# Four changes of order on VectorE and GpSimd in a two-block transformer kernel

## What is computed

```
# first block
z = n @ w_in[l]                                   # n = rms(h)
...
# second block: the recurrence, per head of 128 keys
fg = lbh + (1.0 - lbh) * jax.nn.sigmoid(heads(f, dk))
logf = jnp.log(fg)
kh = 1.0 - fg
...
b = jnp.cumsum(gc, axis=2)
decay = jnp.where(causal, jnp.exp(jnp.where(causal, diff, 0.0)), 0.0)   # diff = b_t - b_s
a = jnp.einsum('bhtd,bhsd,bhtsd->bhts', qc, kc, decay)
o = o_inter + jnp.einsum('bhts,bhsv->bhtv', a, vc)
...
# cross attention
kv = mem @ wkv                                    # mem is normalised first
```

## Time and profile before

| | |
|---|---|
| median of 3 runs | 1199.69 us (1197.97 to 1202.66) |
| profiled execution | 1202.66 us, span 1200.9 us |
| busy | TensorE 97%, VectorE 58%, ScalarE 48%, GpSimd 48% |
| mean granted TensorE clock | 0.992 |
| DMA | 179.38 MB, mean 149 GB/s |
| forget stage | 553.8 to 590.2 us |
| one pass of the head loop | 65.3 us |

### The profile page before, as it was taken

The page is one execution under the profiler, slowest core; times in us unless marked ns, Lnnn a source line. Parts: engine busy times, 40 slices in busy tenths (PEclk is TensorE's granted clock), DMA queues, the critical chain, the costliest instruction groups (busy, mean ns, idle before and its releaser), DMA issues.

```text
span 1200.9 us, 24182 instructions
## 1 busy us (share of the span) xinstructions
PE 1161.5 (97%) x8692; PEld 1099.9 (92%) x8692; DVE 701.1 (58%) x1326; ACT 573.4 (48%) x1083; POOL 580.1 (48%) x415
## 2 busy tenths in 40 slices
PE   4999999999989999999899999999999989999997
PEld 4999999998879999999899989898889979999996
DVE  4684756685647778427775757666556424444323
ACT  5644444454136665447546454554415344544432
POOL 3666667670035666544563637364105205566541
PEclk9999999999989999999999999999999999999998
DMA  7443344444324455633433433333235415545541
GB/s 288 173 141 141 141 153 154 147 145 148 133 106 141 175 175 175 211 141 108 174 121 116 150 105 122 122 140 140 105 141 210 141 67 200 187 177 186 198 142 35
DMA packets 26061, 179.38 MB, mean 149 GB/s; under 512 B 2832, under 2 KB 3984, under 8 KB 4496
## 3 DMA queue, kind: packets, MB, share of 16 engines
q1 hardware_dynamic: 25712, 177.29, 41.4%
q10 hardware_dynamic: 288, 1.26, 0.3%
HBM read 177.49 MB, written 1.05 MB: 149 GB/s over the span
## 4 chain that ended last, share of the span: by engine, by line
PE 82%; DVE 7%; issue 5%; ACT 2%; POOL 2%; DMA 1%; DVEq 0%; POOLq 0%; SPq 0%; ACTq 0%
PE ps L536 47%; PE ps L478 11%; PE ps L773 10%; PE ps L853 2%; POOL parts L407 1%; PE ps L604 1%; DVE ps L1617 1%; PE ps L503 1%; DVE parts L407 1%; PE ps L576 1%; DVE branch L1816 1%; PE ps L846 1%; PE ps L631 1%; PE ps L649 1%; DVE conv L1850 1%
## 5 line engine op out<-in xcount | busy, mean ns | idle before, releaser
L407 POOL TENSOR_TENSOR parts<-ring,parts 128x1024 fp32r<-128x1024 f32 x184 | 452.1, 2465 | 446.3 <-ACT parts L1031 443.3
L536 PE MATMUL ps<-x_high,parts 128*128 128x256 f32 (+2 forms) x3040 | 411.1, 284 | 3.2 <-DVE parts L407 1.3
L536 PEld LDWEIGHTS ps<-x_high,parts 128*128 128x128 f32 x3040 | 380.8, 188 | 14.5 <-issue 9.8
L1031 ACT ACTIVATE parts<-ring 128x1024 fp32r<-128x1024 f32 x296 | 295.9, 1049 | 118.4 <-PE ps L773 66.9
L407 DVE TENSOR_TENSOR parts<-ring,parts 128x1024 fp32r<-128x1024 f32 x112 | 143.5, 1281 | 131.9 <-ACT parts L1031 131.9
L536 PE MATMUL ps<-x_low,parts 128*128 128x256 f32 (+2 forms) x1520 | 214.5, 284 | 0.0
L536 PEld LDWEIGHTS ps<-x_low,parts 128*128 128x128 f32 x1520 | 196.3, 189 | 0.0
L1617 DVE SCALAR_TENSOR_TENSOR ps<-glu,table_sb,ps 128x256 f32<-128x256 f32 x232 | 93.3, 481 | 0.6 <-DVE ps L1617 0.3
L773 PE MATMUL ps<-act_high,parts 128*128 128x256 f32 x704 | 87.8, 279 | 0.0
L773 PEld LDWEIGHTS ps<-act_high,parts 128*128 128x128 f32 x704 | 85.1, 188 | 0.0
L2127 POOL TENSOR_TENSOR sq<-sq 128x256 f32<-128x256 f32 (+1 forms) x18 | 17.2, 956 | 124.2 <-ACT sq L1007 124.0
(11 more groups left out here) (288 smaller groups left out, 1571.0 us busy)
## 6 DMA issues: line engine op xcount, KB each, us to landing
ring<-weights SPq DMA_DIRECT2D x166, 1024.0 KB, 4.8
table_sb<-table ACTq DMA_DIRECT2D x1, 1102.0 KB, 6.1
res<-h_in SPq DMA_DIRECT2D x4, 272.0 KB, 6.2
act<-mem SPq DMA_DIRECT2D x1, 1024.0 KB, 12.8
out<-xT SPq DMA_DIRECT2D x4, 256.0 KB, 2.4
work<-positions ACTq DMA_DIRECT2D x1, 128.0 KB, 3.3
```

The source lines that it names most:

```text
L407: eng.tensor_tensor(parts[:, LOW - HIGH + p, cols], ring[:, slot, cols], parts[:, p, cols].bitcast(F32), ALU.subtract)\
L536: mm = pe.matmul(out, left(k), right(k), start=step_ == 0 and k == 0, stop=step_ == 2 and k == KB - 1)
L1031: sc.activation(parts[:, p, cols], ring[:, slot, cols], ACT.Copy).then_inc(split_high, 1)
```

## The change

Four places change. None changes what is computed, and no instruction is added or removed.

1. In the first head pass, the eight subtractions of the memory's low parts all stand behind `combine1(0)`; before, four stood ahead of `maxima1(0)`.
2. In the forget stage, the low half of a following chunk is made behind the tensor_scalars of tiles 1, 3 and 5 instead of ahead of them.
3. In the head loop, VectorE makes levels 7 and 8 (the second head's first two) right behind low part 5, then both rope steps, and only then `gather1` and `gather2`. Before: `gather1`, rope, `gather2`, levels 7 and 8.
4. GpSimd clears `kl` behind the low half of the head loop's second chunk instead of ahead of it.

```
-            def x_low_parts(dst, src, high, width, name, tiles=range(KB)):
-                for k in tiles:
+            def x_low_parts(dst, src, high, width, name):
+                for k in range(KB):
...
-                else:
-                    x_low_parts(mem_low, k_mem, mem_high, SEQ, "mem", range(4))
                 maxima1(0)
...
                 combine1(0)
                 if earlier is None:
-                    x_low_parts(mem_low, k_mem, mem_high, SEQ, "mem", range(4, KB))
+                    x_low_parts(mem_low, k_mem, mem_high, SEQ, "mem")
...
             for t in range(KB):
-                if t in (1, 3, 5):
-                    low_v("forget" if t < 4 else "heads2", 0, t // 2 + 2 if t < 4 else t // 2 - 2)
                 b = STREAM.bank("forget", t)
...
                 ve.tensor_scalar(bT[:, t, :], bT[:, t, :], LOG_MIN, None, ALU.max).then_inc(forget_ready, 1)
+                if t in (1, 3, 5):
+                    low_v("forget" if t < 4 else "heads2", 0, t // 2 + 2 if t < 4 else t // 2 - 2)
...
                 low_v("heads2", i, 5)
-                gather1()
+                level(i, 1, 7)
+                level(i, 1, 8)
                 rope_sin(2)
                 rope_cos(k_r)
+                gather1()
                 gather2()
-                level(i, 1, 7)
-                level(i, 1, 8)
                 if scan:
...
-            low_g("heads2", 0, 0)
+            for c in range(2):
+                low_g("heads2", 0, c)
             gp.wait_ge(cum_ready, 2)
             gp.memset(kl, 0.0).then_inc(pool_step, 1)
-            low_g("heads2", 0, 1)
             gp.wait_ge(pool_step, n.next(pool_step))
```

## The result

The changed kernel takes 1214.04 us, the median of four runs (1213.07 to 1215.06), against 1200.33 us for the kernel before, the median of four (1197.97 to 1202.66): 13.7 us more, a ratio on record of 1.0117 with a 95% interval of 1.0105 to 1.013. The profiled spans are 1200.9 and 1212.4 us, 11.5 apart. The four runs of the kernel before scatter by 4.7 us, so the difference is not sharp: 71 further runs of that kernel, made beside the experiments on three chips, have a median of 1202.38, and 29 runs of the changed kernel one of 1214.31, 11.9 more, which fits the profiles better than 13.7 does.

What follows compares the result with a forecast made beforehand. TensorE, busy for the whole 65.3 us of a head-loop pass, was taken to bound the kernel. Terms 2.6 + 0.2 + 0 + 9.6 = 12.4 us on the 1199.69 us median gave 1212.1 us, range 1201.5 to 1220.0.

Steps and rivals of the forecast that it cites:

- the likeliest case: Whole kernel: the forecast itself, 1212.1 us, as a case 1209 to 1215 us, chance 0.45.
- Edit 1, +2.6: First head pass: maxima1(1) starts 5.5 us late, probabilities ready at 59.4 against 56.80, 2.6 us slower; bounds 0 and 3.3.
- rival (a): First head pass keeps its slack because VectorE's subtractions go through in one piece: 1209.5 us, chance 0.20.
- rival (d): New TensorE gaps of 2 us bring the low clock: five places, 1.7 us each at most, up to 1220.6; chance 0.12.
- Edit 2, +0.2: Forget stage: first low part delays TensorE 1.8 us, but the 3.34 us gap shrinks to some 2.5; 0.2 us slower.
- The bound on the clock: Forget stage: if the shorter gap spares TensorE the low clock, 1.7 us are given back.
- Edit 4, 0: GpSimd's work behind the memset starts 1.6 us later, covered by slack: cost 0; 1.6 us were that cover gone.
- Edit 3, +9.6: Head loop, four passes: level product held by GpSimd, TensorE 2.5 us late in three passes, 2.1 in the last; bounds 0, 12.8.
- The sum: Whole kernel: 2.6 + 0.2 + 0 + 9.6 = 12.4 us slower, forecast 1212.1 us.
- (b): Head loop: the levels get in ahead of GpSimd, leaving only the first two edits' cost: 1202.5 us, chance 0.08.
- (c): Not slower: neither order costs, and the forget stage's shorter gap spares the low clock: 1198.2 us, chance 0.10.

Runs made afterwards that it cites:

- five, six and seven: Kernel before with five, six or seven memory subtractions behind combine1(0) instead of four: 1202.42, 1202.79 and 1206.55 us, ratios 1.0003, 1.0004 and 1.0038.
- e1_memory: Kernel before with only the memory's eight low-part subtractions all put behind combine1(0): 1207.79 us against 1202.42, ratio 1.005.
- e8b_seven: Kernel before with one memory low part ahead of maxima1(0) and seven behind combine1(0): 1206.55 us against 1202.34, ratio 1.0038.
- e11_early_memset: Kernel before with ScalarE's high parts of the head loop's second chunk made earlier and GpSimd's kl clearing later: 1202.1 us against 1202.34, ratio 0.9998.
- e3_heads: Kernel before with only the head loop's new order, levels 7 and 8 right behind low part 5: 1213.65 us against 1202.42, ratio 1.0086.

## Why the prediction was right, point by point

The forecast was 12.4 us more than before; 13.7 were measured, inside the range, and the likeliest case is the one that came.

- **Edit 1, +2.6.** The stall is 2.8 us, by the steps predicted: counted from the first subtraction at 47.00, the fifth is done at 50.6, the sixth at 53.2, the seventh at 55.7, and maxima1(1) is 5.7 us late against 5.5 said. That GpSimd gets in between VectorE's subtractions, which rival (a) denied, is shown by the steps of 2.5 us with five, six and seven. The term is mis-sized in what comes behind the stall: the slow clock, 1.4 to 1.5 us in three profiled executions (the changed kernel, e1_memory, e8b_seven), which I had put into rival (d). Alone the edit costs 4.7 to 5.4 us by the times, of which the trace accounts for 4.4; the rest stays open.
- **Edit 2, +0.2.** The delay at the first low part was right (1.86 us waited; I said +1.8), and so was its return at the silu2. The gap there shrank to 1.2 us and not to the 2.5 said, because the slow clock behind the stall made TensorE 1.5 us later still, and that was paid back too. The edit is a gain of 3.2 us alone, outside the bounds that I gave it. The bound on the clock, 1.7 us given back, was the outcome and not the exception: I had it as a side of the range and left it out of the sum. 1.5 us of the gain is shown in the trace.
- **Edit 4, 0.** Right: 1.0002. It is free in the old order of ScalarE, where the high parts of that chunk come behind the logarithms: in the changed kernel GpSimd's subtraction starts at 591.21, well behind VectorE's scan at 587.89, and costs nothing although the gap is only 1.21 us. With the chunk made early (e11_early_memset) it meets the scan and takes the whole gain back; I had not counted the scan among the held instructions.
- **Edit 3, +9.6.** Mechanism and place as predicted: 2.49 us for the held product (2.4 said), hgrn_values(0) at 692.30, 1.9 us later over the pass (2.1 said), turn2(0) 2.2 (2.5 said). scores2(0) was 0.1 us late instead of 0.4, because the rope steps ran faster (0.68 and 0.69 us) with GpSimd's differences already done. Without the clock the loop adds 8.4 us, 1.2 less than said; the slow stretch of the third pass, 1.5 us, which was not in the sum, brings it to 9.9. Alone the edit costs 0.86% by the ratio, 11.2 us by the medians.
- **The sum.** That the total came so near is in part luck. The errors had both signs: too little for edit 1 and its clock, too much for edit 2, and in edit 3 stalls taken too long made up for a slow stretch left out. What the forecast got by its mechanism are the two places, the order of the engines there and the length of each stall to within 0.3 us.
- **Rival (d)**, slow stretches behind new gaps, holds in part: the clock fell behind the 2.78 us gap, behind one of the four gaps of 1.74 in the changed kernel, behind two of the four in e3_heads, and behind the 1.86 us stall of the forget stage, where it cost nothing.
- **The rivals (a), (b) and (c)** are excluded by e1_memory and e8b_seven, by e3_heads and by the result. The Trainium skill (SBUF — State Buffer, "Who interferes with whom") says that issue order decides who blocks. The traces agree: at 682.99 GpSimd's subtraction was on record 0.87 us before the product, and went first. I had called that open in the prediction.

## What to carry to other kernels

Where VectorE and GpSimd both read SBUF, look at what VectorE does next after an instruction for which GpSimd is waiting: if it reads two SBUF operands, or is a tensor_scalar from SBUF to SBUF, it was late here by one whole GpSimd subtraction (2.2 us), and if it read PSUM, it was not. So an order of independent steps is worth several times their own length: four 0.28 us products moved ahead of four predicated copies cost 2.3 us a pass here. A stall of the bounding engine should be followed to the next place where it waits anyway; one that lies ahead of such a place is paid back, and a slow stretch of the clock there is too.

## What the runs showed that I had not expected

The scan with two SBUF operands is held by GpSimd as the products are (2.89 us for 1.37). A slow stretch of TensorE's clock can be moved: behind a 1.86 us wait at 569.79 it cost nothing, where the one behind the 3.34 us gap had cost 1.5 us. At the same gap its length differed from one execution to the next: 6.8 us, 3.4 or none. And a GpSimd subtraction of 128 columns is on record for 1.27 us, most of which is its own wait for VectorE, as 3.21 is for 1024 columns where 2.4 is usual: a long record on GpSimd is no sign that it works.
